# Modulation weights of a two-block transformer: sums of scaled pieces moved from VectorE's multiply-adds to ScalarE and accumulating transfers

## What is computed

```python
# c: (1, 1024), w_ada: (2, 1024, 9216), b_ada: (2, 9216)
mod = jax.nn.silu(c) @ w_ada + b_ada    # 2 layers x 9 x 1024 values
# shift, scale and gate of three norms in each layer of the second block
```

## Time and profile before

| | us |
|---|---|
| median of the two runs shown | 3531.49 (3530.07 and 3532.92) |
| profiled execution, first to last instruction (span) | 3529.6 |
| TensorE busy in it | 3498.3 |
| VectorE busy | 2067.0 |
| ScalarE busy | 1307.9 |
| GpSimd busy | 63.8 |

### The profile page before, as it was taken

The page is one execution under the profiler, slowest core; times in us unless marked ns, Lnnn a source line. Parts: engine busy times, 40 slices in busy tenths (PEclk is TensorE's granted clock), DMA queues, the critical chain, the costliest instruction groups (busy, mean ns, idle before and its releaser), DMA issues.

```text
span 3529.6 us, 45935 instructions
## 1 busy us (share of the span) xinstructions
PE 3498.3 (99%) x17160; PEld 2837.1 (80%) x17160; DVE 2067.0 (59%) x3447; ACT 1307.9 (37%) x2145; POOL 63.8 (2%) x122
## 2 busy tenths in 40 slices
PE   9999999999999999999999999999999999999999
PEld 7777777888876788888888887888888887878887
DVE  5777776666876566685334767433443347673334
ACT  5555554222343332333323444323332234442222
POOL 0000000000000000000000000000000000000000
PEclk9999999999999999999999999999999999999999
DMA  4222223656421365652232212323323322223232
GB/s 145 85 65 78 76 65 106 216 200 206 168 71 49 108 200 194 206 187 94 96 95 93 80 66 73 103 99 96 95 90 97 99 91 77 72 73 100 94 101 79
DMA packets 142102, 387.35 MB, mean 110 GB/s; under 512 B 21680, under 2 KB 63024, under 8 KB 141936
## 3 DMA queue, kind: packets, MB, share of 16 engines
q1 hardware_dynamic: 127024, 306.65, 27.1%
q0 software_dynamic: 14912, 78.52, 6.5%
HBM read 382.11 MB, written 2.10 MB: 109 GB/s over the span
## 4 chain that ended last, share of the span: by engine, by line
PE 95%; DVE 3%; issue 1%; ACT 1%; DMA 0%; SPq 0%; DVEq 0%; ACTq 0%
PE psP L1127 26%; PE psP L1132 25%; PE psP L1128 25%; PE psP L1278 3%; PE psP L1285 3%; PE psP L1279 3%; PE psS L1624 1%; PE psM L1647 1%; PE psS L1341 1%; PE psS L1507 1%; PE psS L1310 1%; PE psS L1323 0%; PE psS L1491 0%; PE psS L1329 0%; PE psS L1635 0%
## 5 line engine op out<-in xcount | busy, mean ns | idle before, releaser
L1127 PE MATMUL psP<-h_hi,w_hi 128*128 128x512 f32 x2664 | 1052.5, 395 | 4.8 <-ACT h_hi L734 2.3
L1128 PE MATMUL psP<-h_hi,w_lo 128*128 128x512 f32 x2664 | 1037.7, 390 | 0.0
L1132 PE MATMUL psP<-h_lo,w_hi 128*128 128x512 f32 x2664 | 1027.8, 390 | 0.0
L1740 DVE TENSOR_TENSOR w_lo<-raw,w_hi 128x1024 fp32r<-128x1024 f32 (+1 forms) x456 | 546.7, 1199 | 396.5 <-ACT w_hi L678 390.4
L684 ACT ACTIVATE ybuf<-psP 128x512 f32<-128x512 f32 (+1 forms) x401 | 239.4, 597 | 1199.5 <-PE psP L1132 1198.1
L1127 PEld LDWEIGHTS psP<-h_hi,w_hi 128*128 128x128 f32 x2664 | 500.5, 188 | 127.2 <-issue 25.8
L1132 PEld LDWEIGHTS psP<-h_lo,w_hi 128*128 128x128 f32 x2664 | 498.3, 188 | 107.7 <-DVE h_lo L1818 4.2
L1128 PEld LDWEIGHTS psP<-h_hi,w_lo 128*128 128x128 f32 x2664 | 500.8, 188 | 99.4
L678 ACT ACTIVATE w_hi<-raw 128x1024 fp32r<-128x1024 f32 (+1 forms) x456 | 471.0, 1033 | 65.4 <-PE psP L1132 65.4
L1127 PE MATMUL psP<-a_hi,w_hi 128*128 128x512 f32 x1248 | 486.3, 390 | 1.2 <-ACT a_hi L1080 1.2
L1128 PE MATMUL psP<-a_hi,w_lo 128*128 128x512 f32 x1248 | 485.6, 389 | 0.0
(11 more groups left out here) (336 smaller groups left out, 3545.9 us busy)
## 6 DMA issues: line engine op xcount, KB each, us to landing
raw<-in_gu SPq DMA_DIRECT2D x264, 512.0 KB, 3.3
adaw<-in_ada POOLq DMA_DIRECT2D x96, 768.0 KB, 5.7
raw<-in_down SPq DMA_DIRECT2D x96, 448.0 KB, 3.3
raw<-in_down SPq DMA_DIRECT2D x48, 512.0 KB, 3.6
raw<-in_qkv SPq DMA_DIRECT2D x40, 512.0 KB, 3.6
raw<-in_mix_in SPq DMA_DIRECT2D x34, 512.0 KB, 3.2
raw<-in_qkv SPq DMA_DIRECT2D x64, 256.0 KB, 3.1
raw<-in_wo SPq DMA_DIRECT2D x32, 512.0 KB, 3.3
```

The lines of the kernel that those rows point to most:

```text
L1127: nc.tensor.matmul(psP[:, s, :], hi, rhs[0](kt), start=(n == 0), stop=False)
L1128: nc.tensor.matmul(psP[:, s, :], lo, rhs[0](kt), start=False, stop=False)
L1132: mm = nc.tensor.matmul(psP[:, s, :], w_hi[:, s, kt * P:kt * P + P], rhs[1](kt), start=False, stop=(n == K - 1))
L1740: v.tensor_tensor(w_lo[:, s, 0:cols], raw[:, s, 0:cols], w_hi[:, s, 0:cols].bitcast(F32), ALU.subtract)\
```

## The change

ScalarE gets `ada(c)`: it scales piece c by `cact` in place in the ring (a group's first piece is written to `ada_acc` instead). The sum over a group's other seven pieces is made by transfers from the ring slot to `ada_acc` that add to what lies there, on GpSimd's queue. Each waits until the piece has been scaled and, from the third piece of a group on, until the transfer before has landed. The load of piece c+3 is issued behind the adding transfer of piece c, and waits for that of piece c-1. The loops of ScalarE in F0 and F1 are unrolled, since pieces are placed between tiles. VectorE's `ada` goes; `folded` waits for the transfers, and is placed one pair later in the last part (`ADA_FOLD` 5 in place of 4) and in down tile 6, 6 and 4 (`ADA_LAST`) in place of 4, 4 and 0.

```diff
-ADA_FOLD = (7, 6, 4)
+ADA_FOLD = (7, 6, 5)
+ADA_LAST = (6, 6, 4)
...
+        def added_before(c):
+            return c // KT * (KT - 1) + max(0, c % KT - 1)
...
+            def load_piece(c):
+                pool.dma_start(adaw[:, c % ADA_RING, :], A["ada"][c]).then_inc(ada_landed[c % ADA_RING], 16)
...
-                for c in range(F.ada * 48, F.ada * 48 + 48):
-                    pool.wait_ge(ada_used, c + 1)
-                    pool.dma_start(adaw[:, c % ADA_RING, :], A["ada"][c]).then_inc(ada_landed[c % ADA_RING], 16)
+                first, end = F.ada * 48, F.ada * 48 + 48
+                for c in range(first, first + ADA_RING - 1):
+                    load_piece(c)
+                for c in range(first, end):
+                    if c % KT:
+                        pool.wait_ge(ada_scaled, c + 1)
+                        if c % KT > 1:
+                            pool.wait_ge(ada_added, 16 * added_before(c))
+                        pool.dma_start(ada_acc[:, c // KT % 2, :], adaw[:, c % ADA_RING, :], accum_op=ALU.add).then_inc(ada_added, 16)
+                    if c + ADA_RING - 1 < end:
+                        if c > first:
+                            if (c - 1) % KT:
+                                pool.wait_ge(ada_added, 16 * added_before(c))
+                            else:
+                                pool.wait_ge(ada_scaled, c)
+                        load_piece(c + ADA_RING - 1)
...
+            def ada(c):
+                g, kt = divmod(c, KT)
+                w = adaw[:, c % ADA_RING, :]
+                act.wait_ge(ada_landed[c % ADA_RING], (c // ADA_RING + 1) * 16)
+                if kt == 0 and g >= 2:
+                    act.wait_ge(ada_folded, g - 1)
+                nc.scalar.activation(w if kt else ada_acc[:, g % 2, :], w, copy, scale=cact[:, kt:kt + 1]).then_inc(ada_scaled, 1)
...
                     for j in range(rest):
                         evac(ACT.Silu if j % 2 == 0 else copy)
                         hi(2, shapes[j + 3])
+                        for _ in range(ADA_PAIRS[n][j // 2]) if F and j % 2 else ():
+                            ada(c_ada)
+                            c_ada += 1
...
                         if shapes[rest + m + 3] and not ends:
                             hi(2, shapes[rest + m + 3])
+                        if F and m < ADA_DOWN[n]:
+                            ada(c_ada)
+                            c_ada += 1
...
             def folded(g):
-                dve.wait_ge(ada_used, ADA_RING + (g + 1) * KT)
+                dve.wait_ge(ada_added, 16 * (g + 1) * (KT - 1))
...
-                    dve.wait_ge(ada_landed[c % ADA_RING], (c // ADA_RING + 1) * 16)
-                    dve.wait_ge(ada_used, c + ADA_RING)
-                    if kt == 0:
-                        i = v.tensor_scalar(total, w, at, None, ALU.mult)
-                    else:
-                        i = v.scalar_tensor_tensor(total, w, at, total, ALU.mult, ALU.add)
-                    i.then_inc(ada_used, 1)
...
-                            if m < ADA_DOWN[n]:
-                                ada(c_ada)
-                                c_ada += 1
-                            elif m == ADA_DOWN[n]:
+                            if m == ADA_LAST[n]:
                                 folded(g + 1)
```

More of the change, by code:

```diff
@@ L461, in program @@
         cact_ready = sem("cact_ready")
-        ada_used = sem("ada_used")
+        ada_scaled = sem("ada_scaled")
+        ada_added = sem("ada_added")
         ada_folded = sem("ada_folded")
@@ L740, in rotation, with ffn @@
                 nc.scalar.activation(rope2[:, :], ang[:, :], ACT.Sin).then_inc(sin_ready, 1)
-            def ffn(l, N, next_l, nxt, gate_col=None, after_second=None):
+            def ada(c):
[5 more added lines that the diff above has]
+                nc.scalar.activation(w if kt else ada_acc[:, g % 2, :], w, copy, scale=cact[:, kt:kt + 1]).then_inc(ada_scaled, 1)
+            def ffn(l, N, next_l, nxt, gate_col=None, after_second=None, F=None):
                 for n, (f0, nf) in enumerate(PARTS):
@@ L745, in ffn @@
                         after_second()
[L746 to L750, removed]
+                    rest = 2 * nf
+                    c_ada = None if F is None else (F.ada * len(PARTS) + n) * 2 * KT
+                    if F is None:
+                        with tile_loop(act, pos, nf // 3, 6):
+                            for j in range(6):
+                                evac(ACT.Silu if j % 2 == 0 else copy)
+                                hi(2, D)
+                        rest = 2 * (nf % 3)
                     after = (D, D, D) if n + 1 < len(PARTS) else nxt
@@ L797, in _ @@
             act.wait_ge(r_tok_ready, 1)
+            act.wait_ge(cact_ready, 1)
             def phases_of(k):
@@ L911, in _ @@
             norm(N_ffn0, 0, h_split[0])
-            ffn(0, N_gla, 0, (D, D, D))
+            ffn(0, N_gla, 0, (D, D, D), F=F0)
             norm(N_gla, 0, h_split[0])
@@ L983, in _ @@
             norm(N_ffn1, 0, h_split[0])
-            ffn(0, N_f1, 0, (D, D, D), after_second=rotation)
+            ffn(0, N_f1, 0, (D, D, D), after_second=rotation, F=F1)
             for l in range(2):
@@ L1921, in ffn @@
             def ffn(F, l, N, nxt, after_first=None, gate_col=None):
-                def ada(c):
-                    g, kt = divmod(c, KT)
-                    w, total, at = adaw[:, c % ADA_RING, :], ada_acc[:, g % 2, :], cact[:, kt:kt + 1]
-                    dve.wait_ge(ada_landed[c % ADA_RING], (c // ADA_RING + 1) * 16)
-                    dve.wait_ge(ada_used, c + ADA_RING)
-                    if kt == 0:
-                        i = v.tensor_scalar(total, w, at, None, ALU.mult)
-                    else:
-                        i = v.scalar_tensor_tensor(total, w, at, total, ALU.mult, ALU.add)
-                    i.then_inc(ada_used, 1)
                 for n, (f0, nf) in enumerate(PARTS):
@@ L1937, in ffn @@
                     if g is not None:
-                        c_ada = g * KT
                         if n == 0:
@@ L1949, in ffn @@
                         gated(a_at(nf - rest + j), F, l * FT + (f0 + nf - rest + j), shapes[2 * j + 3:2 * j + 5])
-                        for _ in range(ADA_PAIRS[n][j]) if g is not None else ():
-                            ada(c_ada)
-                            c_ada += 1
                         if g is not None and j == ADA_FOLD[n]:
@@ L1974, in _ @@
             v.memset(credit[:, 2:3], 0.0).then_inc(gmix_ready, 1)
-            v.memset(credit[:, 3:4], 0.0).then_inc(ada_used, ADA_RING)
             for k, started in enumerate((mix_ready, F0.a_ready, F1.a_ready, F2.a_ready, F3.a_ready, o1_ready)):
@@ L2148, in _ @@
             norm(N_ffn0, 0, lambda m: pc("ffn_norm", m))
-            dve.wait_ge(cact_ready, 1)
             def gates_split():
```

## The result

| | before | after |
|---|---|---|
| median of the runs | 3531.49 (2 runs) | 3627.24 (3625.14 and 3629.34) |
| span of the profiled execution | 3529.6 | 3627.5 |

The ratio is 1.0272, with a 95% interval of 1.0254 to 1.0289: 96 us slower, where 33 were forecast and 2% is 71. The direction was as forecast, the size was not: 3627 lies outside the likeliest case (3531 to 3602) and inside the range.

What follows compares the result with a forecast made beforehand. TensorE was taken to bound the kernel (busy 3498.3 of 3529.6 us). Freed VectorE and added ScalarE work counted 0, waits for adding transfers 16.6 us in F0, repeated in F1: 33, so 3565 on the median; 8-in-10 range 3527 to 3765.

Steps and rivals of the forecast that it cites:

- the likeliest case: The forecast itself: period of the adding transfers 6.3 to 8.2 us, time 3531 to 3602, likeliest 3565; chance 0.33.
- VectorE's freed time is worth nothing: The 164 us removed from VectorE lie beside TensorE's work and gain 0; rival of over 2% faster, 0.02.
- ScalarE's scalings are free: 96 scalings of 128x1536 on ScalarE, 1.45 us each, add nothing on the path.
- The adding transfer is two readings and a fixed part: On GpSimd's queue: 3.7 us of the engines for two readings, 2.45 fixed, 0.29 to issue; alone 6.4.
- L = 7.5: Period in us between adding transfers' issues on GpSimd's queue: 0.29 + 2.45 + 4.8; bounds 4.6 and 9.9.
- fits just so: The next piece's load, 2.4 us behind the adding transfer in GpSimd's queue, falls in the fixed part of 2.7.
- The loss by parts: Waits for a part's 14 adding transfers in F0: last 16.2 us, middle 0.4, first none; F1 repeats F0.
- the formulas: Loss in us, L being the period: last part 14L-88.8, middle 14L-104.6, first 14L-118.
- ScalarE stands for pieces in the last part, inside the fold's loss: Piece 16, due at 928, lands at about 946; TensorE stops some 12 us, inside the fold's 16, not added.
- The signs: Profile should show: landing 7.2 us, issues 7.5 apart in last parts, VectorE idle 16 before transpose, first part without wait.
- three units: Rival, chance 0.28: an adding transfer's readings and writing don't overlap, period 9.9 us; both feed-forwards lose 209, time 3740.
- a slow adder: Rival, chance 0.19: the adder or descriptor making is slow, period 12.3 us; 205 lost in a feed-forward, time 3941.

Runs made afterwards that it cites:

- the even spread: The full change with the last part's 16 pieces spread as 2 behind each pair and 2 behind the first down tiles: 3632.7 us, ratio 1.0295.

## Why the prediction was right or wrong

- *VectorE's freed time is worth nothing*: right, shown by the run in which VectorE adds.
- *ScalarE's scalings are free*: right; they took 1.575 us against 1.45 estimated, and without adding transfers the time is that of before.
- *The adding transfer is two readings and a fixed part*: right. Engine work 3.7 forecast, 3.7 to 3.8 measured alone; fixed part with the issue 2.74 forecast, 2.3 measured; alone 6.4 forecast, 6.0 measured.
- *L = 7.5*: too small. This is the term that failed, and it was too small in three places:
  - The landing. Forecast were 7.2 us; the median is 7.4, but a chain pays the mean, 7.7. The step behind it was that the main loads stretch the engines' part (3.7/0.77) while the next piece's load "fits just so" in the fixed part. The runs with small loads show 6.1 with both streams small. The main loads add 0.8 to that, where the forecast had 1.1, and the piece loads add 0.7, where it had nothing.
  - The issue. From a landing to the next adding transfer passed 0.52 us, not 0.29, the value of a row with one wait; the new queue has two in a row there. That the second wait makes the difference was not tried.
  - ScalarE. The prediction let 14 transfers run at L from the first issue on, as if the next scaled piece were always there. Yet piece 2 is scaled a pair behind piece 1. In the run with both loads small, where no stall stands at this border, the second transfer comes 9.4 us behind the first:

```profile
749.65 0.90 POOL L677 DMA_DIRECT2D ada_acc<-adaw  x1 [17.99 <-ACT adaw L774]
...
759.06 0.87 POOL L677 DMA_DIRECT2D ada_acc<-adaw  x1 [7.96 <-ACT adaw L774]
```

  In the change's first part the third comes 10.9 us behind the second, and the second group's first 12.0 behind the last of the first group, both released by ScalarE.
- *The loss by parts*: the formulas were right, and they are steep: at 7.5 almost only the last part loses, a little higher all three do. In the change the second transfer of a part comes 13 to 20 us behind the first in place of 9.4, since the fold of the part before has stopped TensorE and with it ScalarE. This lateness costs nothing of its own: at the first border the second transfer is 8.6 us late, and so is TensorE's next tile (ScalarE empties it 759.24 - 745.22 = 14.0 us after the one before, not 5.44), so the chain and the work that it will hold up move together. Without it the six chains took 114 to 125 us, 118 in the mean or 8.46 a transfer. For each chain's own length the formulas give 48 us in F0 and 39 in F1, 88 in all (with the median's 7.9 it would have been 56). The first part loses 6.5 by its 124.5 us, where no wait was forecast; the wait measured there is 5.5. ScalarE's two emptyings at the first border:

```profile
745.22 0.60 ACT L707 ACTIVATE ybuf<-psP 128x512 f32<-128x512 f32 x1 [3.89 <-PE psP L1174]
...
759.24 0.60 ACT L707 ACTIVATE ybuf<-psP 128x512 f32<-128x512 f32 x1 [9.55 <-PE psP L1174]
```

- *The clock*: missing altogether. Its slow starts come to 20 us. Most of them fall ahead of a wait for a chain, and shorten it by as much; the three that stand between a part's fold and the next part's second transfer, 2.9, 2.2 and 1.8 us, delay the path and the chain alike and come on top. This division is an estimate from the rows.
- The sum is then: 33 forecast at L = 7.5; 55 more by the longer chains; about 7 by the clock. That makes 95 of the 98 us between the spans; the last 3 stay open.
- *ScalarE stands for pieces in the last part, inside the fold's loss*: right for the full change (the even spread gives nothing), and a loss of its own, 13 us, where the chain has room.
- *The signs*: the landing (7.2 forecast, 7.4 median) came, but the issues were 9.2 us apart in the mean of F0's last part, not 7.5. VectorE did not stand before the transpose in down tile 4, where 16 us were forecast: ScalarE's late pieces held it before that. And the first part had a wait where none was forecast.
- *The two rivals for slower, together 0.47, by three units or a slow adder*: slower came true, but by neither cause.

## What to carry to other kernels

Before work is moved off an engine, ask whether TensorE waits for that engine at all: here 159 us of VectorE were worth nothing. A transfer that adds in place is paid for twice on the DMA engines, and a chain of them must be priced with every other load that runs meanwhile and with the order in which its inputs come, by the mean of its periods and not by the median: here about one microsecond more for each transfer turned 33 us of loss into 88. If the sum of all work nears the engines' full share, more transfers in flight help little (18 of 96 us). Where the busiest engine is TensorE, a short stall can be dearer than it looks, by the clock behind it.

## What was not expected of the hardware

- Behind four stalls of 6.7 us put into the kernel before, TensorE's granted clock fell to 0.50 and its matmuls started at half the pace for 4.4 to 6.0 us, 2.4 us of loss a stall. In the kernel before it was 1.00 all through F0. In the kernel after, such a stretch followed ten of fifteen waits, the shortest of them 2.0 us long.
- An adding transfer's issue occupied GpSimd for 0.86 us, a plain one's for 0.53, and in the full kernel 0.52 us passed from a landing to the next issue where alone it was 0.29.
- Eight adding transfers in flight wrote 206 GB/s, eight copies 418: half within 2%, at a share of 1.0 in both.
